# Modulation blocks 8 to 23 summed by VectorE, and the first loads in another order

## The reference, cut to what matters

```
h = rms_norm(x, norm_ffn_g)
x = x + square(relu(h @ ffn_w1)) @ ffn_w2      # 2048 -> 8192 -> 2048
```

```
mod = silu(c) @ ada_w + ada_b                  # 2048 -> 12288
h * (1 + scale) + shift                        # modulate
```

## Time and profile before

| | |
|---|---|
| median of three runs | 3230.01 us |
| profiled execution, own time | 3229.23 us |
| its span | 3227.4 us |
| mean granted TensorE clock | 0.986 |
| TensorE busy | 3089.8 us, 96% |
| VectorE busy | 1917.2 us, 59% |
| ScalarE busy | 1415.5 us, 44% |
| GpSimd busy | 244.4 us, 8% |
| bytes moved | 620 MB, 192 GB/s in the mean |

### The profile page before, as it was taken

One profiled execution on the slowest core, in us unless ns is written; L12 is line 12 of the kernel. 1 busy time (PEld: TensorE's weight loads), 2 busy tenths in 40 slices (PEclk: granted clock), 3 DMA queues, 4 the chain that ended last, 5 costly groups with the idle time before them and its releaser, 6 DMA issues.

```text
span 3227.4 us, 54438 instructions
## 1 busy us (share of the span) xinstructions
PE 3089.8 (96%) x22670; PEld 2696.5 (84%) x22670; DVE 1917.2 (59%) x2598; ACT 1415.5 (44%) x1994; POOL 244.4 (8%) x203
## 2 busy tenths in 40 slices
PE   7999989899999999999999999999998999999998
PEld 6898978787888888888788889988877888888887
DVE  5475763543755785555555565345667666666666
ACT  4343442433544573444434454343425445444443
POOL 1100321020100110000000230010001000000002
PEclk9999999999999999999999999999999999999999
DMA  6554555546644666777777777763434566656654
GB/s 213 177 159 132 156 177 198 189 157 207 228 153 148 205 191 191 230 253 241 256 246 253 249 242 239 252 187 115 159 104 147 173 205 182 187 180 194 187 177 146
DMA packets 535783, 620.07 MB, mean 192 GB/s; under 512 B 19451, under 2 KB 459926, under 8 KB 534177
## 3 DMA queue, kind: packets, MB, share of 16 engines
q1 hardware_dynamic: 527008, 586.51, 57.7%
q0 software_dynamic: 3344, 23.78, 2.1%
q10 hardware_dynamic: 5184, 6.29, 0.6%
HBM read 608.12 MB, written 8.39 MB: 191 GB/s over the span
## 4 chain that ended last, share of the span: by engine, by line
PE 78%; DVE 4%; ACT 2%; DMA 2%; issue 1%; POOL 0%; SPq 0%; ACTq 0%; DVEq 0%; POOLq 0%
PE psum L591 35%; PE psum L592 18%; PE psum L563 3%; PE psum L566 3%; PE psum L565 3%; PE psum L691 3%; PE psum L1749 2%; PE psum L625 2%; PE psum L627 2%; PE psum L628 2%; DVE wlo L520 1%; DMA wraw<-in_ffn_w 1%; PE psum L675 1%; PE psum L2398 0%; PE psum L1940 0%
## 5 line engine op out<-in xcount | busy, mean ns | idle before, releaser
L513 ACT ACTIVATE whi<-wraw 128x1024 fp32r<-128x1024 f32 (+1 forms) x948 | 977.7, 1033 | 1203.7 <-PE psum L592 455.4
L520 DVE TENSOR_TENSOR wlo<-wraw,whi 128x1024 fp32r<-128x1024 f32 (+1 forms) x948 | 1150.8, 1226 | 559.6 <-ACT whi L513 552.6
L591 PE MATMUL psum<-g,whi 128*128 128x512 f32 x2816 | 1000.9, 397 | 15.8 <-issue 8.2
L591 PE MATMUL psum<-h,whi 128*128 128x512 f32 x2240 | 793.4, 396 | 5.0 <-DVE h L2037 2.4
L592 PE MATMUL psum<-g,wlo 128*128 128x256 f32 x2816 | 788.3, 280 | 0.0
L591 PEld LDWEIGHTS psum<-g,whi 128*128 128x128 f32 x2816 | 530.5, 188 | 162.9 <-issue 25.9
L592 PE MATMUL psum<-h,wlo 128*128 128x256 f32 x2240 | 633.6, 283 | 0.0
L592 PEld LDWEIGHTS psum<-g,wlo 128*128 128x128 f32 x2816 | 530.7, 188 | 0.5
L591 PEld LDWEIGHTS psum<-h,whi 128*128 128x128 f32 x2240 | 421.2, 188 | 122.9 <-issue 21.9
L592 PEld LDWEIGHTS psum<-h,wlo 128*128 128x128 f32 x2240 | 421.7, 188 | 0.2
L563 PE MATMUL psum<-h,whi 128*128 128x256 f32 x1040 | 304.3, 293 | 35.1 <-DVE h L896 22.0
(11 more groups left out here) (468 smaller groups left out, 3368.2 us busy)
## 6 DMA issues: line engine op xcount, KB each, us to landing
wraw<-in_ffn_w SPq DMA_DIRECT2D x256, 512.0 KB, 6.7
wraw<-in_w_in SPq DMA_DIRECT2D x204, 512.0 KB, 4.7
wraw<-in_ada_w SPq DMA_DIRECT2D x192, 512.0 KB, 4.8
wraw<-in_ffn_w_up SPq DMA_DIRECT2D x160, 512.0 KB, 4.5
wraw<-in_w_out SPq DMA_DIRECT2D x64, 512.0 KB, 4.5
wraw<-in_ffn_w_down SPq DMA_DIRECT2D x64, 512.0 KB, 4.6
wraw<-in_xattn_wk SPq DMA_DIRECT2D x32, 512.0 KB, 4.5
wraw<-in_xattn_wv SPq DMA_DIRECT2D x32, 512.0 KB, 4.6
```

What stands on the lines that cost most here:

```text
L513: e.activation(high(i), view(WRAW[i % NR], i), ACT.Copy).then_inc(*hi.up(i))
L520: e.tensor_tensor(low(i), view(WRAW[i % NR], i), high(i).bitcast(F32), SUB).then_inc(*lo.up(i))
L591: e.matmul(both_of(g, j), w_hi[:, kk, s:s + 128], X[:, k, :], start=k == 0, stop=False, skip_group_check=True)
```

## The change

- The plan of ada2: nothing beside the first products; behind every four chunks of each of the four second products (dn0 too, now) three modulation chunks instead of two. 4 x 8 x 3 = 96 chunks, the same twelve blocks. In ada3 one chunk stands behind every two instead of two behind every four.
- Blocks 8 to 23 are no longer multiplied by TensorE. VectorE multiplies each of the two rows-of-128 of a chunk by its column of silu(c) and adds it into an accumulator of 128 x 2 x 512 (`rows_v`), two operations a chunk, and adds the two halves after the eighth chunk. These chunks are `summed`: SyncE waits for VectorE's sum before it refills their buffer.
- TensorE's gather multiplies the accumulator, 128 columns at a time, with two columns of ones (`gather_p`). Only c is used, both columns of `MOD` get it. ScalarE's copy is gone. The accumulators (two, by parity of n) lie in `CX`.
- `mats` is asked for by ScalarE behind x instead of by SyncE ahead of the weights; the engines wait for it later; GpSimd asks for the filters when x's last piece has landed.
- The last gather moves behind q2's start, and one wait of GpSimd is for modulation 23 instead of the inner norm.

```diff
-WC = 4
+WC = 2
-def weave(main, extra, per):
+def weave(main, extra, per, times=1):
         if n % per == 0:
-            for other in islice(extra, 2):
+            for other in islice(extra, times):
                 yield other
...
                     plain.add(len(chunks) - 1)
+                    if n >= NA0:
+                        summed.add(len(chunks) - 1)
...
-        woven = plan_ada("ada2", NA0, NA2)
+        woven = plan_ada("ada2", NA0, 20)
         for i in range(4):
-            made(weave(plan(f"up{i}", ...), woven if i else iter(()), WF))
-            made(weave(plan(f"dn{i}", ...), woven if i else iter(()), WF))
+            made(plan(f"up{i}", ...))
+            made(weave(plan(f"dn{i}", ...), woven, WF, 3))
...
+        def rows_v(e, n, ci, ids, acc):
+            a, (i, k0, m), before = acc[:, n % 2, :, :], ids[ci], ids[ci - 1][0]
+            if ci == 0 and n > NA0 + 1:
+                e.wait_ge(*ada.p.at("mod", n - 2))
+            landed(e, i)
+            if ci:
+                e.wait_ge(*ada.v.at("sum", before))
+            for kk in range(2):
+                w, by = view(WRAW[i % NR], i)[:, kk, :], SF[:, k0 + kk, 0:1]
+                if ci == 0:
+                    x = e.tensor_scalar(a[:, kk, :], w, by, None, MUL)
+                else:
+                    x = e.scalar_tensor_tensor(a[:, kk, :], w, by, a[:, kk, :], MUL, ADD)
+            x.then_inc(*ada.v.up(("sum", i)))
+            if ci == 7:
+                e.wait_ge(*ada.v.now())
+                e.tensor_tensor(a[:, 0, :], a[:, 0, :], a[:, 1, :], ADD).then_inc(*ada.v.up(("acc", n)))
+
+        def mod_v(e, name, acc, lo_to, weight=None):
+            for n, ids in PL[name]:
+                for ci, (i, k0, m) in enumerate(ids):
+                    lo_to(e, reach(i, 2))
+                    if ci == 6 and n > NA0:
+                        modulation_v(e, n - 1)
+                    rows_v(e, n, ci, ids, acc)
+                    yield weight
+
+        def gather_p(e, n, acc):
+            e.wait_ge(*ada.v.at("acc", n))
+            for j in range(4):
+                x = e.matmul(PSUM[:, ada_bank(n), 2 * j:2 * j + 2], acc[:, n % 2, 0, 128 * j:128 * j + 128], ones[:, 0:2], start=True, stop=True)
+            x.then_inc(*ada.p.up(("mod", n)))
+
+        def mod_p(e, name, acc, weight=None):
+            for n, ids in PL[name]:
+                for ci in range(8):
+                    if ci == 2 and n > NA0:
+                        gather_p(e, n - 1, acc)
+                    yield weight
...
         def sync(e):
             e.dma_start(PK[:, :], A_["pack"]).then_inc(*d_pk.up("all"))
-            e.dma_start(MT[:, :], A_["mats"]).then_inc(*d_mt.up("all"))
             for i in range(len(chunks)):
                 j = i - NR
-                if j in plain:
+                if j in summed:
+                    e.wait_ge(*ada.v.at("sum", j))
+                elif j in plain:
                     e.wait_ge(*mm.at("chunk", j))
...
         def gpsimd(e):
             ada_first_g(e)
+            e.wait_ge(*d_x0[3].at("all"))
             load_filters(e)
```

More of the change, by code:

```diff
@@ L28 @@
 ROUT = 1.5
-NA2 = 20
 CN = 512
@@ L658, in ada_first_a @@
                 e.dma_start(X0[:, 4 * g:4 * g + 4, :], A_["x"][:, 4 * g:4 * g + 4, :]).then_inc(*d_x0[g].up("all"))
+            e.dma_start(MT[:, :], A_["mats"]).then_inc(*d_mt.up("all"))
             sf = SF[:, :, :].rearrange("p k m -> p m k")
@@ L2503, in tensor @@
         def tensor(e):
-            e.wait_ge(*d_mt.at("all"))
-            side = Side(sums_p(e, fn, TM1, False, 0.3), idle(1), spectrum_p(e))
+            side = Side(then(lambda e: e.wait_ge(*d_mt.at("all")), e), sums_p(e, fn, TM1, False, 0.3), idle(1), spectrum_p(e))
             side.beside(gemm_p(e, PL["in_ssd"], [(HH, HL)], lambda e, k: e.wait_ge(*fn.v.at("lo", k // 4))), RSPEC)
@@ L2539, in tensor @@
                     xat.ended(e)
[L2540 to L2543, removed]
+                side.beside(gemm_wide_p(e, PL[f"up{i}"], GX, lambda e, k: None if i else e.wait_ge(*res.v.at("lo", "xo", k)),
+                                              (lambda e, ci: ci == 3 and factor_p(e, "xo", ACC[:, :])) if i == 0 else None))
                 side.beside(weave(gemm_wide_p(e, PL[f"dn{i}"], HX, lambda e, k: e.wait_ge(*ff1.v.at("lo", i, k))),
-                                  here, WF))
-                if i == 3:
-                    made(extra)
+                                  extra, WF, 3))
+            made(extra)
             side.rest()
@@ L2616, in vector @@
             extra = ada_v(e, "ada1", lo_to, WA)
-            side.beside(weave(stream(e, lo_to, 2, PL["xk"], xk_evac_v), extra, WK), RW)
-            side.beside(weave(tok_stream(e, lo_to, 2, PL["xv"], 2, last=lambda e, ci: ci and mix_v(e, ci - 1)), extra, WV), RW)
+            side.beside(weave(stream(e, lo_to, 2, PL["xk"], xk_evac_v), extra, WK, 2), RW)
+            side.beside(weave(tok_stream(e, lo_to, 2, PL["xv"], 2, last=lambda e, ci: ci and mix_v(e, ci - 1)), extra, WV, 2), RW)
             made(extra)
@@ L2679, in vector @@
             made(extra)
-            side = Side()
+            side = Side(idle(5), then(lambda e: modulation_v(e, 23), e))
             for b in range(2):
@@ L2732, in scalar @@
                 x_high(e, g)
-            side = Side(sums_a(e, fn, X0, TM1, RS1[:, :], None, 0.3), then(fn.ended, e), spectrum_a(e))
+            side = Side(idle(1), sums_a(e, fn, X0, TM1, RS1[:, :], None, 0.3), then(fn.ended, e), spectrum_a(e))
             side.beside(stream(e, hi_to, 3, PL["in_ssd"], None, gate_a), RSPEC)
@@ L2783, in scalar @@
                                         lambda j: MOD[:, j, 1:2], lambda e: e.wait_ge(*d_cx.at("all"))))
-            extra = ada_a(e, "ada2", MO4, hi_to, WA)
+            extra = mod_a(e, "ada2", hi_to, WA)
             for i in range(4):
-                here = extra if i else iter(())
                 if i == 1:
@@ L2789, in scalar @@
                     ctx.ended(e)
-                side.beside(weave(stream(e, hi_to, 3, PL[f"up{i}"], lambda e, g, q, t, what: up_evac_a(e, i, g, q, t, what),
-                                         lambda e, t: up_post_a(e, i, t), xo_carry if i == 0 else None),
-                                  here, WF))
+                side.beside(stream(e, hi_to, 3, PL[f"up{i}"], lambda e, g, q, t, what: up_evac_a(e, i, g, q, t, what),
+                                         lambda e, t: up_post_a(e, i, t), xo_carry if i == 0 else None))
                 side.beside(weave(stream(e, hi_to, 3, PL[f"dn{i}"], None, (lambda e, t: both_squares_a(e, t)) if i == 3 else None,
                                          lambda e, ci: ci < 2 and up_post_a(e, i, 14 + ci)),
-                                  here, WF))
-                if i == 3:
-                    made(extra)
+                                  extra, WF, 3))
+            made(extra)
             side.rest()
```

71 lines of the change are left out of this document (35 added, 36 removed).

## The result

| | before | after |
|---|---|---|
| median | 3230.27 us (4 runs, 3219.39 to 3234.20) | 3321.38 us (4 runs, 3319.20 to 3325.78) |
| ratio | | 1.0289 (95%: 1.0262 to 1.0317) |
| span of the profiled execution | 3227.4 us | 3318.1 us |
| mean granted TensorE clock | 0.986 | 0.969 |

What follows compares the result with a forecast made beforehand. TensorE, busy for 96%, was taken as the bound. Span 3227.4 + 57 (feed-forward) - 19 (k2c to v2x) - 9 (start) = 3256, forecast as 3258 us; range 3216 to 3292.

Steps and rivals of the forecast that it cites:

- What bounds the kernel, what is removed: Whole kernel: TensorE bounds it and loses 76.8 us of work, 57.6 in the feed-forward and 19.2 beside k2c to v2x.
- The loop: Second products: six transfers, a high half, a low half and a sum before the next release; period 15.2 us against TensorE's 11.2.
- the sixth at 11.8: Second products: the period's sixth transfer lands 11.8 us after the first sum's end, with second and third issued singly.
- The sum over the feed-forward: Four second products lose 28.6 us each, 114 together, against 57.6 paid before: feed-forward 57 us longer.
- The clock: Second products: half clock after waits of about 3 us, hidden inside periods, costing 1.7 us at the end.
- the clock would stay low: Rival, second products: four chunks at half clock take 22.4 us, +224 and over 3450 us; chance 0.03.
- TensorE 70 to 80% busy: Sign in windows over the second products, with some 118 us for each instead of 99.
- k2c to v2x: Last four blocks: the loop just closes at 11.4 us for two periods, so 19.2 us are won, bounds 10 and 19.2.
- The start: First loads reordered: first weights at 7 to 8 us, TensorE at 12 to 14 instead of 22, 9 us won.
- The loop does not bind: Rival, second products: transfers overlap more and VectorE's work fits; 3144 us, or 3170 at 12 us a period; chance 0.12.
- at its lower end: Second rival, second products: the loop binds at a period of 14.2 to 14.7 us, 3222 to 3238 us; chance 0.2.
- T of 16 to 17: Rival, second products: sums over 1.6 us or later adds give periods of 16 to 17 us, 3281 to 3309; chance 0.12.

Runs made afterwards that it cites:

- e1: The changed kernel, but VectorE sums the three modulation chunks of a period ahead of the low halves of the next product chunks: 3166.29 us, ratio 0.9805.
- e5: e1 with the modulation chunks of the twelve feed-forward blocks at their old places (two behind every four product chunks, up1 to dn3): 3160.21 us, ratio 0.9771.
- e11: e1 with blocks 8 to 21 two chunks behind every four from dn0 to dn3, blocks 22 and 23 beside v2c and k2x: 3148.48 us, ratio 0.9761.
- e2: (e2_burst) The changed kernel, with SyncE waiting for the third sum so that six transfers leave in one burst: 3350.43 us in one run.
- e6: The changed kernel, with VectorE making one low half less ahead of the sum: 3275.43 us, ratio 1.0128.
- e3: The kernel before, with only the new order of the first loads (mats behind x, filters behind x's last piece): 3222.09 us, ratio 0.9970.
- e8: e1 with the first loads in the order of the kernel before: 3170.10 us, ratio 0.9807.

## Why the prediction was right in its mechanism and wrong in its size

**What bounds the kernel, what is removed.** Right, and a little too small. With the waits gone (e1, e5, e11) TensorE is the bound again. Before, the feed-forward stood 73.5 us over 64 periods of 11.2 (716.8), not 57.6: the woven first products were 14 us over, not 9.6. Those 16 us went as well.

**The loop (the step that failed).** The loop is the one drawn, link by link, and e1, e2 and e6 show it by changing the order, the issues and the last transfer. The term mis-sized is "the sixth at 11.8": it landed at 12.4 to 14.1, 13.3 in the mean of 28 periods. The rest was right: high half 1.06, low half 1.23, sum 1.43, together 3.7 to 3.8. The first two landings were as said too (3.7 and 6.0, against 3.7 and 6.1). The third is where it went: at 8.7 and not 7.4, 2.5 behind the second where I had put 1.4. The fourth came 1.7 behind it, not 1.4, the last two 1.5 each, as said. I had charged the gap of a single issue once, and the third issue is apart as well. Why such an issue lands that much later is not shown.

A part of the miss was in the trace of before. My 10.8 for a burst came from one burst (third at 6.8, fifth at 9.8) and from tables 1.38 apart. The 47 bursts of before's feed-forward that have two tables and four product chunks would by these prices end at 11.1; their sixth lands at 11.6 in the mean. The change's own six in a burst land at 11.6 as well (e2_burst), not at 10.8. So of the 1.5 us that the sixth came late, 0.8 lay in the burst and 0.7 in the single issues, which cost 1.7 and not 1.0. 17.1 against 15.2 is 13.3 us in each second product: 28.6 + 13.3 = 41.9, and the four took 163.6 over 4 x 89.6, 40.9 each.

The Trainium skill (DMA: Bandwidth & Descriptors, Anatomy of one DMA) gave 13.0 us for the period by its fixed part and rate. The trace has 17.1, so the measurement decides; the section writes of GpSimd's path, and these are SyncE's transfers.

**The sum over the feed-forward.** +92.8 against +57: 52 more from the loop (166.3 over the floor for the eight stages, 114 forecast), 16 less by the term above.

**The clock.** Right in kind. Nearly once a period, most often behind a wait of 2.5 to 3.4 us, TensorE was granted 0.50 for one stretch of 3.4 us, and 0.92 in the mean of a second product. One wait, what followed it, and what followed that:

```profile
1469.65:1472.35 2.70, 0.00 (x1) 0.00 (x0) 2.63 (x6) 1.06 (x1) 0.00 (x0) 1.00 0.93 294
1472.44:1475.85 3.41, 3.41 (x11) 2.93 (x12) 0.99 (x1) 0.00 (x0) 0.00 (x0) 0.50 0.95 311
1475.85:1480.00 4.15, 4.15 (x28) 3.68 (x26) 0.86 (x1) 1.54 (x2) 0.00 (x0) 1.00 0.89 305
```

The sixth landing (13.3) and the 3.7 us behind it already make the whole period of 17, so the loss lies under the loop's own wait. That the clock would stay low is refuted. The sign "TensorE 70 to 80% busy" came out at 84%, as a matmul at half clock counts as busy.

**k2c to v2x.** Wrong at one place. v2c, k2x and v2x together are 15.7 us shorter, all of three times 4.8 and a little more: the loop closes there as forecast, and the last window above shows it. k2c is 12.9 longer instead of 4.8 shorter. VectorE at its entry in after:

```profile
1987.48 1.23 DVE L520 TENSOR_TENSOR wlo<-wraw,whi 128x1024 fp32r<-128x1024 f32 x1 [0.19 <-ACT whi L513]
1988.63 1.41 DVE L745 SCALAR_TENSOR_TENSOR cx<-wraw,sf,cx 128x512 f32<-128x512 f32 x2
...
1990.14 2.93 DVE L745 SCALAR_TENSOR_TENSOR cx<-wraw,sf,cx 128x512 f32<-128x512 f32 x4
...
1993.71 1.67 DVE L1914 TENSOR_TENSOR xt<-psum,xt 128x256 f32<-128x256 f32 x4
```

and TensorE's first matmul of k2c (the wait ahead of it in brackets):

```profile
1995.48 0.55 PE L563 MATMUL psum<-chi,whi 128*128 128x256 f32 x1 [10.63 <-DVE xt L1914]
```

dn3's last adds stand behind the last three sums, which stand behind low halves. TensorE's last matmul of dn3 starts at 1984.57, and k2c needs the adds: 10.63 us of wait. The clock fell during it, and stayed low for the first 6.0 us of work, of which half (3.0) is lost:

```profile
1987.90:1995.48 7.58, 0.00 (x1) 0.03 (x1) 7.35 (x14) 1.92 (x4) 0.36 (x1) 0.50 0.47 145
1995.48:2001.50 6.02, 6.02 (x28) 6.02 (x29) 4.42 (x4) 2.28 (x4) 4.63 (x4) 0.50 0.79 252
```

That is 13.6 us at the exit of dn3, where I had put nothing; the miss is 17.7. The rest lies further on: up to v2c's first matmul TensorE waits five more times for low halves, 6.1 us together.

That rest is the inner norm's side, which I had named as a danger, and without the exit's wait it costs more. In e1 the wait is 4.44 us and k2c still takes 62.9. In e5 and in e11 TensorE waits the same 1.28 us at the exit. From its first matmul of k2c to its first of v2c it then takes 57.5 us with sums beside it (e5, first row) and 47.0 without (e11, second row):

```profile
1839.05:1896.55 57.50, 49.80 (x397) 49.28 (x397) 47.05 (x55) 33.27 (x49) 3.82 (x4) 0.97 0.65 208
...
1834.85:1881.86 47.01, 47.01 (x389) 46.91 (x389) 33.40 (x30) 31.80 (x46) 4.42 (x4) 1.00 0.65 196
```

So both are there: removing the exit's wait alone uncovers the norm's.

**The start.** Right for TensorE's first matmul; what it is worth for the whole is less sure. In after, ScalarE's first high half came a little later than forecast, TensorE's first matmul in time (forecast 7 to 8, and 12 to 14; the earlier trace rows had 17.52 and 22.02):

```profile
9.18 1.06 ACT L513 ACTIVATE whi<-wraw 128x1024 fp32r<-128x1024 f32 x1 [3.22 <-DMA wraw<-in_w_in]
```

```profile
13.68 0.55 PE L563 MATMUL psum<-h,whi 128*128 128x256 f32 x1 [13.68 <-DVE h L946]
```

Nine us were forecast and e3 has ten, by its interval 6 to 13. In after's profiled execution the lead was 10.4 us at in_rwkv and gone at xq, which lies within the spread of that stretch (e8). It makes up the last 9 of the 62 us between the forecast span of 3256 and 3318.

**The rivals.** "The loop does not bind" and "at its lower end" fell with T = 17.1. "T of 16 to 17" was nearest in kind (second products 34 to 41 us over), though its causes were not the ones: a sum costs 1.43 us, and the adds are where they were. The range ended at a T of 16 since its bounds for the landing charged one late issue, where the schedule has two, and took the burst from a single one. (The second rival's sum is 2 us off: 80 to 96 against 57.6, less 28, is 3224 to 3240; nothing hangs on it.)

## What to carry to other kernels

When an engine takes over the release of a ring's buffers, write down the loop from that release over the issue, the landings and back, in the order of the releasing engine's own queue: work of later chunks that stands ahead of the release is paid in full, even with VectorE, ScalarE and the DMA engines under 70%. First put the release ahead of the work that looks further on (155 us here, for some ten lines), and then look at what the exits and entries of a stage wait for. And cost transfers as they will be issued: apart by the pace of the releases, not in a burst, and from the mean of many periods, not from one.

## What the runs showed of the hardware

- Six transfers of 512 KB, the second and third issued 1.5 us apart behind the first and the rest at 3.5 to 5.8 us, land in the mean 3.7, 6.1, 8.7, 10.3, 11.9 and 13.3 us after the first issue. The same six, issued within 2.7 us, land at 3.8, 5.2, 7.1, 8.6, 10.1 and 11.6 (means of 28 periods each).
- A product-and-add of 128x512 float32 with one number per partition: 747 ns in the mean, six in 4.45 us, so 0.74 each; a chunk 1.43 to 1.48 us.
- The DMA engines carried 310 GB/s at a share of 0.95 beside a VectorE busy for 92% and a TensorE busy for all of 80 us at a granted clock of 1.00 (e1).
- Most of TensorE's waits of 2.5 to 3.4 us in the second products were followed by 3.4 us at a granted clock of 0.50. Within the wait of 10.63 us the granted clock fell to 0.50, and it stayed there for the first 6.0 us of work behind it.
- The stretch ahead of xo differs by 8 to 9 us between profiled executions of programs that are equal there, as much as the start's whole gain.
